# A 64-block expert loop: one more eighth of each gate and up product in split form, and two re-orderings around it

## The reference

```
a  = silu(xb @ w_gate[e]) * (xb @ w_up[e])        # 1024 -> 256, twice
yb = (a @ w_down[e]) * wt[:, None]                # 256 -> 1024
acc = acc.at[tok].add(yb)
```

## Time and profile before

| | |
|---|---|
| median of 3 runs | 1110.73 us (1109.42 to 1127.9) |
| profiled execution | 1109.17 us, span 1107.4 us |
| busy share of the span | PE 96%, PEld 72%, DVE 68%, ACT 58%, POOL 24% |
| granted clock of TensorE, mean | 0.982 of full speed |
| bytes moved | 299.02 MB, 270 GB/s over the span |
| largest groups on PE | split gate and up 267.7 us and more (line 1920), down 165.0 us and more (line 1954), whole slices 61.9 us and more (line 1933) |

### The profile page before, as it was taken

How to read it: one execution, slowest core, us unless ns; L and a number is a source line. 1 busy time by engine, 2 the same in 40 slices (tenths; PEclk the granted TensorE clock), 3 DMA queues, 4 the chain that set the end, 5 groups by cost and what they waited for, 6 DMA issues and landing times.

```text
span 1107.4 us, 17623 instructions
## 1 busy us (share of the span) xinstructions
PE 1061.4 (96%) x5991; PEld 796.5 (72%) x5991; DVE 748.3 (68%) x1332; ACT 646.5 (58%) x850; POOL 262.8 (24%) x180
## 2 busy tenths in 40 slices
PE   5999999999999999999999999999999999999991
PEld 5999458999669888666667666766667666766660
DVE  4733834633934575787788777887788778887762
ACT  4374343432643313677767776677767776677662
POOL 1001320000000101233333333333333333333321
PEclk8999999999999899999999999999999999999996
DMA  9500336050953525899999999999999999999945
GB/s 300 225 4 31 142 143 229 1 229 27 379 211 157 227 79 192 288 359 375 368 367 369 368 377 363 351 357 357 364 366 369 359 356 358 369 367 374 361 113 172
DMA packets 64342, 299.02 MB, mean 270 GB/s; under 512 B 12591, under 2 KB 15227, under 8 KB 39718
## 3 DMA queue, kind: packets, MB, share of 16 engines
q1 hardware_dynamic: 49102, 261.93, 61.7%
q0 software_dynamic: 15200, 36.55, 13.4%
HBM read 281.34 MB, written 34.00 MB: 285 GB/s over the span
## 4 chain that ended last, share of the span: by engine, by line
PE 90%; DMA 3%; DVE 3%; ACT 2%; SPq 1%; issue 1%; POOLq 0%; ACTq 0%; DVEq 0%
PE pair L1920 23%; PE pair L181 18%; PE pair L1954 16%; PE pair L1933 10%; PE pair L1659 5%; PE pair L1905 5%; PE pair L1562 3%; PE pair L1940 1%; DMA regA<-in_w_in 1%; PE pS L1868 1%; PE pair L1752 1%; PE pair L1760 1%; PE pS L1731 1%; DMA acc_rows<-regL 1%; DMA regL<-h_rows,regL 1%; DVE regL L1113 1%
## 5 line engine op out<-in xcount | busy, mean ns | idle before, releaser
L1920 PE MATMUL pair<-w_hi,h_parts 128*96 128x512 f32 x768 | 267.7, 430 | 0.0
L715 POOL DMA_INDIRECT acc_rows<-regL x64 | 93.0, 1453 | 389.8 <-ACT regL L1032 275.2
L1920 PEld LDWEIGHTS pair<-w_hi,h_parts 128*96 128x96 f32 x768 | 121.5, 165 | 69.7 <-issue 33.9
L1954 PE MATMUL pair<-w_hi,act_parts 128*96 128x512 f32 x512 | 165.0, 404 | 2.6 <-DVE act_parts L1509 2.6
L706 POOL DMA_INDIRECT regL<-h_rows,regL x65 | 139.7, 2148 | 74.7 <-DVE regL L1351 49.4
L1032 ACT ACTIVATE regL<-pair,regL 96x1024 f32<-96x1024 f32 x64 | 71.1, 1110 | 125.0 <-PE pair L1954 125.0
L1455 DVE TENSOR_TENSOR lo_A<-regA,w_hi 128x1536 fp32r<-128x1536 f32 x64 | 111.9, 1749 | 0.2 <-ACT w_hi L992 0.2
L1954 PEld LDWEIGHTS pair<-w_hi,act_parts 128*96 128x96 f32 x512 | 80.2, 167 | 29.9 <-issue 2.8
L992 ACT CAST w_hi<-regA 128x1536 fp32r<-128x1536 f32 x64 | 94.7, 1482 | 0.0
L1505 DVE TENSOR_TENSOR lo_B<-regB,w_hi 128x2048 fp32r<-128x2048 f32 x32 | 73.4, 2293 | 29.6 <-ACT w_hi L1027 29.6
L1505 DVE TENSOR_TENSOR lo_A<-regA,w_hi 128x2048 fp32r<-128x2048 f32 x32 | 73.4, 2292 | 24.7 <-ACT w_hi L1027 24.7
(11 more groups left out here) (344 smaller groups left out, 2207.3 us busy)
## 6 DMA issues: line engine op xcount, KB each, us to landing
regA<-in_exp_w_gate SPq DMA_DIRECT2D x32, 1024.0 KB, 9.1
regA<-in_exp_w_up SPq DMA_DIRECT2D x32, 1024.0 KB, 12.2
regA<-in_exp_w_down SPq DMA_DIRECT2D x32, 1024.0 KB, 14.0
regB<-in_exp_w_down SPq DMA_DIRECT2D x32, 1024.0 KB, 15.3
regB<-in_exp_w_gate SPq DMA_DIRECT2D x16, 1024.0 KB, 10.0
regB<-in_exp_w_up SPq DMA_DIRECT2D x16, 1024.0 KB, 13.6
regC<-in_exp_w_gate SPq DMA_DIRECT2D x16, 1024.0 KB, 9.2
regC<-in_exp_w_up SPq DMA_DIRECT2D x16, 1024.0 KB, 12.6
```

Source lines behind the costliest of these rows:

```text
L715: pool.indirect_dma_start(acc_rows, bass.IndirectOffsetOnAxis(ap=kept[0:SLOTS, r, 0:1].bitcast(U32), axis=0), yX[r][0:SLOTS, :], None, bou ...
L1920: ins = pe.matmul(out, x, w, start=False, stop=half == 1 and k == CUT_K - 1 and s == 2, skip_group_check=True)
L1954: ins = pe.matmul(pair[2][0:SLOTS, h, :], act_parts[:, x, k, :], w[:, k, cols], start=k == 0 and s == 0, stop=k == KF - 1 and s == 2)
```

## The change

- WHOLE_K goes from 2 to 1: of the 8 slices one is a whole product and 7 are split, 3 in the first half (slices 1 to 3) and 4 in the second (slices 4 to 7). Each row half of the turned activations now has all 4 of its slices in `h_parts`; `hX` holds one slice.
- The high part of the down weights moves out of `w_hi` into `wd_parts`, which lies over the tail of `rows`. So ACT now waits, ahead of the loop, until the start sums have landed (`sums_landed`).
- POOL's scatter in the step of block b is that of b-3 in place of b-2: the gather of b+2 then stands in front of the scatter of b-2. Three scatters are left behind the loop, not two.
- Behind the loop ACT cuts the last down weights first, ahead of `at` of the block before and of the last `silu`, and DVE subtracts them ahead of the last `gate`.

```
-WHOLE_K = 2
-CUT_K = (KD - WHOLE_K) // 2
-CUT = CUT_K * 256
+WHOLE_K = 1
+CUT_KS = (range(WHOLE_K, KD // 2), range(KD // 2, KD))
+CUT = (KD - WHOLE_K) * 256
...
+        with nc.sbuf_tensor("unused_L4", [P, 4160], F32), nc.sbuf_tensor("wd_parts", [P, KF * D], F32R) as wd_parts:
...
-        WD_hi = view(w_hi, 3072, KF, D)
+        WD_hi = view(wd_parts, 0, KF, D)
...  POOL, step_of_block
                 gather((j + 1) % PAIR, (j + 1) % RING, b + 1)
-                if not (peeled and j < 2):
-                    scatter((j - 2) % RING, b - 2)
+                if not (peeled and j < 3):
+                    scatter((j - 3) % RING, b - 3)
...
-            for left in (2, 1):
+            for left in (3, 2, 1):
...  ACT, cut_up
-                k0 = WHOLE_K + half * CUT_K
-                a.copy(WG_hi[r % 2][:, half], WG[r][:, :, k0 * FE:(k0 + CUT_K) * FE]).then_inc(wg_hi, 1)
+                lo, hi = CUT_KS[half][0] * FE, (CUT_KS[half][-1] + 1) * FE
+                a.copy(WG_hi[r % 2][:, :, lo - WHOLE_K * FE:hi - WHOLE_K * FE], WG[r][:, :, lo:hi]).then_inc(wg_hi, 1)
...  ACT, turn
-                a.copy(hX[:, :, :], pair[1][:, :, 0:SLOTS])
-                a.copy(h_parts[:, 0], pair[1][:, :, SLOTS:(1 + CUT_K) * SLOTS]).then_inc(turned_a, 1)
+                a.copy(hX, pair[1][:, 0, 0:SLOTS])
+                a.copy(h_parts[:, 0], pair[1][:, :, 0:KD // 2 * SLOTS]).then_inc(turned_a, 1)
...  ACT, ahead of the loop
             for t in range(NTT):
                 start_sums(t)
+            a.wait_ge(sums_landed, 16 * NTT)
...  ACT, behind the loop
+            cut_down(RING - 1, last, n_turns, last_hi)
             at(last - 1)
             silu(last)
             table(ACT.Sqrt)
-            cut_down(RING - 1, last, n_turns, last_hi)
...  DVE, behind the loop
             at(last - 1)
+            cut_down(RING - 1, last, last_hi)
             gate(last)
             keep(RING - 1, last)
-            cut_down(RING - 1, last, last_hi)
```

More of the change, by code:

```diff
@@ L234, in sem @@
             return ctx.enter_context(nc.semaphore(name))
-        with nc.sbuf_tensor("w_hi", [P, 8192], F32R) as w_hi:
+        with nc.sbuf_tensor("w_hi", [P, 8320], F32R) as w_hi:
             pass
@@ L264, in trunk @@
             pass
-        with nc.sbuf_tensor("unused_L3", [P, 10872], F32), nc.sbuf_tensor("h_parts", [P, 2, 2, CUT_K * SLOTS], F32R) as h_parts:
+        with nc.sbuf_tensor("unused_L4", [P, 4160], F32), nc.sbuf_tensor("wd_parts", [P, KF * D], F32R) as wd_parts:
+            pass
+        with nc.sbuf_tensor("unused_L3", [P, 10872], F32), nc.sbuf_tensor("h_parts", [P, 2, 2, KD // 2 * SLOTS], F32R) as h_parts:
             pass
@@ L399, in trunk @@
         gath = [view(regL, 8824 + D * j, D) for j in range(PAIR)]
-        hX = view(regL, 12024, WHOLE_K, SLOTS)
+        hX = view(regL, 12408, SLOTS)
         places = view(regL, 14200, 112)
@@ L408, in trunk @@
         WD_lo = [view(lo_A, 4096, KF, D), view(lo_A, 10240, KF, D), view(lo_B, 4096, KF, D), view(lo_B, 6144, KF, D)]
-        WG_hi = [view(w_hi, 5120, 2, 2, CUT), view(w_hi, 0, 2, 2, CUT)]
-        last_hi = view(w_hi, 5120, KF, D)
+        WG_hi = [view(w_hi, 4160, 2, CUT), view(w_hi, 0, 2, CUT)]
+        last_hi = view(w_hi, 4160, KF, D)
         sdw_hi, sdw_lo = WD_lo[3], view(lo_C, 4096, KF, D)
-        WD_hi = view(w_hi, 3072, KF, D)
+        WD_hi = view(wd_parts, 0, KF, D)
         yf = view(regA, 0, NTT, D)
@@ L1452, in cut_up @@
                 v.wait_ge(wg_hi, 2 * b + half + 1)
-                k0 = WHOLE_K + half * CUT_K
-                cols = slice(k0 * FE, (k0 + CUT_K) * FE)
-                v.tensor_tensor(WG_lo[r][:, :, cols], WG[r][:, :, cols], WG_hi[r % 2][:, half].bitcast(F32),
+                lo, hi = CUT_KS[half][0] * FE, (CUT_KS[half][-1] + 1) * FE
+                v.tensor_tensor(WG_lo[r][:, :, lo:hi], WG[r][:, :, lo:hi],
+                                WG_hi[r % 2][:, :, lo - WHOLE_K * FE:hi - WHOLE_K * FE].bitcast(F32),
                                 ALU.subtract).then_inc(wg_lo, 1)
@@ L1494, in turn @@
                 v.wait_ge(turned_a, b + 1)
-                v.tensor_tensor(h_parts[:, 1], pair[1][:, :, SLOTS:(1 + CUT_K) * SLOTS], h_parts[:, 0].bitcast(F32),
+                v.tensor_tensor(h_parts[:, 1], pair[1][:, :, 0:KD // 2 * SLOTS], h_parts[:, 0].bitcast(F32),
                                 ALU.subtract).then_inc(turned_d, 1)
@@ L1903, in turn @@
                 for k in range(KD):
-                    h, n = (k, 0) if k < WHOLE_K else ((k - WHOLE_K) // CUT_K, 1 + (k - WHOLE_K) % CUT_K)
+                    h, n = k // (KD // 2), k % (KD // 2)
                     ins = pe.transpose(pair[1][:, h, n * SLOTS:(n + 1) * SLOTS], g3[0:SLOTS, k, :], ident[0:SLOTS, 0:SLOTS])
@@ L1910, in gate_up @@
                 out = pair[0][0:SLOTS, 0, :].rearrange("p (s f) -> p s f", s=2)
-                hi = WG_hi[r % 2][:, half].rearrange("p s (k f) -> p s k f", k=CUT_K)
+                hi = WG_hi[r % 2].rearrange("p s (k f) -> p s k f", k=KD - WHOLE_K)
                 lo = WG_lo[r].rearrange("p s (k f) -> p s k f", k=KD)
@@ L1915, in gate_up @@
                     pe.wait_ge(turned_d, b + 1)
[L1916 to L1920, removed]
+                for k in CUT_KS[half]:
+                    n = k % (KD // 2)
+                    x_hi, x_lo = (h_parts[:, x, half, n * SLOTS:(n + 1) * SLOTS] for x in range(2))
+                    for s, (x, w) in enumerate(((x_hi, hi[:, :, k - WHOLE_K, :]), (x_lo, hi[:, :, k - WHOLE_K, :]), (x_hi, lo[:, :, k, :]))):
+                        ins = pe.matmul(out, x, w, start=False, stop=k == KD - 1 and s == 2,
                                         skip_group_check=True)
@@ L1932, in gate_up_whole @@
                 for k in range(WHOLE_K):
-                    pe.matmul(pair[0][0:SLOTS, 0, :].rearrange("p (s f) -> p s f", s=2), hX[:, k, :], w[:, :, k, :],
+                    pe.matmul(pair[0][0:SLOTS, 0, :].rearrange("p (s f) -> p s f", s=2), hX, w[:, :, k, :],
                               start=k == 0, stop=False, skip_group_check=True)
```

## The result

The changed kernel is a little slower: 1111.78 us median (20 runs, 1108.57 to 1115.74) against 1109.64 us for the kernel before on the same chip (20 runs). The ratio is 1.0024, with an interval of [1.0013, 1.0036]. It lies inside the range of the prediction and on the other side of no change from its 1109. In some of the series a few executions are slow ones; ratios and intervals leave these out, medians do not. The execution whose trace is read here took 1114.14 us, span 1112.4. It is one of the longer ones, so differences read from it are larger than that of the medians.

A forecast was written before the change was run, and what follows sets the result against it. PE was taken to bound the loop, with transfers close behind. From 1109.17 us, -0.03 (PE's first split product after the last weights) + 0.69 (three more products) - 0.93 (the end) = -0.3 gave 1109 us; range 1101 to 1114.

The forecast's parts named there:

- The slice that became split: In the loop: PE's lap falls from 9.97 to 9.84 us, 0.13 gained a lap, with DVE just making the hand-over.
- Rival 2: In the loop: DVE becomes the bound with a lap of 10.71 us, 48 us more, 1157 us; chance 0.05.
- The new wait of ACT: Ahead of the loop: ACT waits for the start sums until 447.7 us, making block 6's weights some 4.0 us late.
- 4.58 - 0.85 + 0.69 - 0.13: At the start: PE's later first split product, less an absorbed gather wait, plus three products, less one lap's gain; given as 4.0.
- rival 3: At the start: PE's products after its standstill run slow, 1.8 to 3.6 us, nothing won back, 1112 to 1114 us; chance 0.1.
- What the transfers then allow: Weight stream from 466 us: its end comes 0.7 to 4.0 us late, and PE's gain turns into waiting for weights.
- the middle: Last up weights: taken as 2.35 us late, landing at 1062.35, between winning back 3.3 us and nothing.
- Rival 1: In the loop: the transfers keep up with PE to the end, 4.9 us gained, 1104 us, at best 1101; chance 0.25.
- The gather ahead of the scatter: POOL's order in the loop: gather some 3 us earlier, scatter about 1 us later; gain and cost both nothing.
- The end: Behind the loop: DVE's last down-weight subtraction moves ahead of the gate, 0.93 us gained.
- up to 1.8 more: PE's last down products: a shorter gap may keep PE's clock, gaining up to 1.8 us more; not counted.
- The 24.7 us: End of the loop before the change: last up weights' landing time, read as transfers 15 us behind PE, 1.1 us left.

The follow-up runs named there:

- the order alone: Kernel before with only POOL's order changed (scatter of block b-3 behind the gather of b+1, three scatters behind the loop): 1108.87 us, ratio 0.9984.
- the wait alone: Kernel before with only ACT's wait for the start sums added ahead of the loop: 1117.13 us, ratio 1.0044.
- The runs without rows: Row index bound set to 0, so nearly nothing is gathered or added: changed kernel 1101.31 us, with ACT's wait moved later 1097.91, kernel before 1103.78.
- the late wait: Changed kernel with ACT's wait for the start sums moved to just ahead of its first cut of down weights: 1108.71 us (0.9983), later 1106.16 (0.9972).
- the late wait and the old order: Changed kernel with ACT's wait moved to its first down-weight cut and POOL's scatter of b-2 again in the step of b: 1113.58 us, ratio 1.0036.
- the old end: Changed kernel, ACT's wait moved to its first down-weight cut, last down-weight cuts of ACT and DVE put back: 1106.48 us (0.9965), then 1106.03 (0.9971).
- the end alone: Kernel before with only the last down weights cut ahead of the last silu on ACT and last gate on DVE: 1108.85 us, ratio 0.9986.

## Why the prediction was wrong

**The slice that became split: right.** The lap is 9.85 (9.84 expected), DVE's 0.79 us wait for ACT is down to 0.18, and its turn just makes the hand-over. Rival 2 is out: PE shows no waits in the first windows.

**The new wait of ACT: the place right, the price short, and near it by chance.** ACT's cuts start at 447.96 (447.7 expected), PE's first split product at 455.18 (455.2 expected). The agreement is in part chance: this execution was 0.9 us behind before the loop began, and counted from there both came 0.6 to 0.9 us sooner than forecast. Then that product and the eight after it went at 1.2 GHz and took 1.6 us more. Counted from the shared expert's down products, block 6's weights were 4.7 us late, not 4.0 (5.6 on the clock of the trace). The terms of the forecast, 4.58 - 0.85 + 0.69 - 0.13, add up to 4.3 and not to 4.0; the 0.9 too much ahead of the product and the 1.6 left out behind it stood against each other. The prediction had the slow products as rival 3, from the row of the last down product, and left them out of the sum.

**What the transfers then allow: this is the step that failed.** The sum took the middle, 2.35 us late, between a stream that wins back 3.3 us and one that wins back nothing; the last up weights landed 6.1 late (5.2 counted from the shared expert's down products). The reason given for the middle, that the transfers kept 9.97 until 700 us without falling behind and so might keep a shorter lap too, was wrong. They were always busy at a share of 1.02, and with a lap of 9.85 they fell behind from the start, to landings of 13.4 us at the median before 700. Nor do they always keep 9.97: at that lap landings before 700 were 11.3 us at the median with the order alone and 15.8 with the wait alone. The runs without rows show that it is this resource, and the table shows that the stream's length does not follow the lap. So nearly all of the loop's gain on PE was turned into waiting, as foreseen in kind; the late start was not won back, as not foreseen. Rival 3 with its 1112 to 1114 has both halves, and the median lies at its edge. The forecast was 0.3 us of gain; the medians have 2.1 us of loss.

Rival 1 is out with it. Where weights stream almost alone, from 465 to 470 us, the kernel after moves 421 GB/s at a share of 1.00; in its loop, with the rows' packets among them, 364 to 368 at 1.02. On its page of the profile the queue with the rows takes 13.4% for 36.55 MB and the one with the weights 61.1% for 261.93 MB: 1.6 times the time for a byte. The Trainium skill ("DMA: Bandwidth & Descriptors", section Bandwidth) has 425 GB/s on one core for a large load; the short window agrees with it, the loop does not reach it.

**The gather ahead of the scatter: "nothing" was wrong, though it cost the sum little.** The prediction priced the move at the lap of before, where it is worth 0 to 3.5 us. A scatter's cycle is its landing and some 0.9 until the next issue. In the kernel before that is 8.6 + 0.9 = 9.5 us at the median, half a microsecond under the lap. With the late wait and the old order the chain of waits goes through six scatters, from 503.03 to 566.86: 10.6 us a cycle at the mean, with landings of 8.9 to 10.7, above either lap. The gather behind each came late, and PE waited for it. Why scatters landed later there than before is not shown; the two longest cycles are those of scatters that took 3.4 us to issue (see the last section). With the order moved this cost the sum nothing in the loop; a forecast of the slice alone would have missed about 6 us. What the prediction put at nothing and was not is the wait of each scatter for the one before, at the end of the program.

**The end: a size wrong, and hidden.** PE's end gained 2.5 us and not 0.93: the granted clock was 1.00 from 1080 to 1085 us behind the gap of 1.68, and 0.69 before behind one of 2.61. The prediction named this "up to 1.8 more" and did not count it. With POOL's old order 1.6 of the 2.5 reached the last scatter; in the changed kernel, for the reason that the prediction gave, the last scatter waits for the one before, 2.94 us behind ACT, and beside the old end nothing is seen of the gain.

**What stays open.** Streams with the same loop differ by 5 us and more (593.2 before, 587.9 with the end alone, 600.7 with the wait alone, all at a lap of 9.97), each in one trace; no run here shows why. The 24.7 us on which the forecast rested was one such draw, and the 17.7 and 19.4 of the order alone and the end alone would have promised 5 to 7 us more room. Open too is what the 2 to 4 us consist of by which the late wait beats the kernel before.

## What to carry to other kernels

Where the DMA share is 1 and landings still look short, the transfers may be the bound already, and a shorter lap of the engine then buys little (here 1 to 2 us of 6.8): count the stream's own length, from a first issue to a last landing, and compare it with what the engine's laps need. In this loop a stall ahead of the stream was paid in full at the end, so put a new wait where its data is first needed. And before shortening a lap, look for every cycle that closes just under it (here a scatter's, 9.5 us at the median), as an order that costs little at one lap can cost some 6 us at the next. Before two traces are subtracted, compare a point ahead of the edit in both: here 0.9 us of 5.6 were there.

## What the runs showed that was not expected

An indirect transfer on POOL can take much longer to issue beside a long subtraction of DVE. In the changed kernel without rows (timeline of DVE and POOL):

```profile
703.24 2.29 DVE L1508 TENSOR_TENSOR lo_A<-regA,wd_parts 128x2048 fp32r<-128x2048 f32 x1 [0.21 <-ACT wd_parts L1029]
...
703.34 3.51 POOL L717 DMA_INDIRECT acc_rows<-regL  x1 [0.30 <-issue]
```

It ends at 706.85, 1.32 us after the subtraction; with no subtraction beside it a scatter takes 1.42 to 1.45. It matters when the two start: one that began 0.63 us ahead of such a subtraction took 1.45 too (711.56). In the kernel after, one from 719.07 to 722.93 ends 1.33 us behind a subtraction that ended at 721.60. The kernel before had its gathers there, 2.03 us where one of the kernel after takes 0.98; the change put its scatters there, 1.95 us at the mean in place of 1.45. The Trainium skill ("SBUF — State Buffer", section Who interferes with whom) says that a DVE instruction with two SBUF inputs and a GpSimd instruction that reads SBUF exclude each other. These rows agree with it: both of the subtraction's inputs lie in SBUF, and so do the indices. That the indices' reading is what waits was not tried.
